# The conditioning table of the first stage in parts of 512 columns, four tiles at a time

## The reference

```python
cond = jax.nn.silu(c)                        # c: (1, 1024)
for l in range(DEPTH):
    mod = cond @ w_ada[l] + b_ada[l]         # w_ada[l]: (1024, 9 * 1024)
    sh1, sc1, g1, sh2, sc2, g2, sh3, sc3, g3 = jnp.split(mod, N_MOD, axis=-1)
    h = modulate(rms_norm(x), sh1, sc1)
    x = x + 0.5 * g1[:, None, :] * swiglu(h, w_ff1_in[l], w_ff1_out[l])
    ...
```

## Time and profile before

| | |
|---|---|
| median of 3 runs | 3588.3 us (3585.97 to 3589.84) |
| span of the profiled execution | 3586.1 us |
| PE busy | 3451.8 us (96%) |
| DVE, ACT, POOL busy | 1818.5, 1210.8, 643.6 us |
| moved by DMA | 357.82 MB, 100 GB/s in the mean |
| the table's 16 parts | 512 KB each, 8.7 us from issue to landing (median) |

### The profile page before, as it was taken

The page is one execution under the profiler, slowest core; times in us unless marked ns, Lnnn a source line. Parts: engine busy times, 40 slices in busy tenths (PEclk is TensorE's granted clock), DMA queues, the critical chain, the costliest instruction groups (busy, mean ns, idle before and its releaser), DMA issues. The chain is left out here.

```text
span 3586.1 us, 49320 instructions
## 1 busy us (share of the span) xinstructions
PE 3451.8 (96%) x20618; PEld 2725.1 (76%) x20618; DVE 1818.5 (51%) x2601; ACT 1210.8 (34%) x1729; POOL 643.6 (18%) x438
## 2 busy tenths in 40 slices
PE   7999999989999999999998899999899999989999
PEld 5888774577888788877558688878678887778887
DVE  6777536745454566663574533336643335363332
ACT  4222334544222322233364422232542223253223
POOL 4202111131202120211013120220021210001112
PEclk9999999999999999999999999999999999999999
DMA  7565321003443346542000223222132223123321
GB/s 232 162 208 170 124 72 36 7 27 105 128 154 116 120 155 198 157 137 84 32 10 27 83 88 107 87 87 83 36 106 94 95 94 97 48 71 96 104 94 59
DMA packets 445201, 357.82 MB, mean 100 GB/s; under 512 B 15990, under 2 KB 441012, under 8 KB 444980
## 3 DMA queue, kind: packets, MB, share of 16 engines
q1 hardware_dynamic: 444980, 354.67, 31.5%
HBM read 350.43 MB, written 2.10 MB: 98 GB/s over the span
## 5 line engine op out<-in xcount | busy, mean ns | idle before, releaser
L600 DVE TENSOR_TENSOR ring_wlo<-ring_raw,ring_whi 128x2048 fp32r<-128x2048 f32 (+3 forms) x268 | 570.8, 2130 | 377.2 <-ACT ring_whi L581 346.5
L581 ACT ACTIVATE ring_whi<-ring_raw 128x2048 fp32r<-128x2048 f32 (+3 forms) x278 | 490.4, 1765 | 649.3 <-PE f_ps L1099 242.9
L1097 PE MATMUL f_ps<-act_hi,ring_whi 128*128 128x512 f32 x1280 | 502.0, 392 | 2.5 <-DVEq L1251 2.5
L1099 PE MATMUL f_ps<-act_hi,ring_wlo 128*128 128x512 f32 x1280 | 498.7, 390 | 0.0
L1098 PE MATMUL f_ps<-act_lo,ring_whi 128*128 128x512 f32 x1280 | 498.0, 389 | 0.0
L1207 POOL TENSOR_TENSOR f_glo<-f_v,f_ghi 128x512 fp32r<-128x512 f32 x88 | 237.7, 2701 | 1035.2 <-ACT f_ghi L1199 1035.2
L1189 ACT ACTIVATE f_t<-f_ps 128x512 f32<-128x512 f32 x88 | 52.6, 598 | 692.8 <-PE f_ps L1099 648.4
L1097 PEld LDWEIGHTS f_ps<-act_hi,ring_whi 128*128 128x128 f32 x1280 | 240.3, 188 | 52.3 <-DVEq L1251 3.8
L1099 PEld LDWEIGHTS f_ps<-act_hi,ring_wlo 128*128 128x128 f32 x1280 | 240.2, 188 | 50.7
L1098 PEld LDWEIGHTS f_ps<-act_lo,ring_whi 128*128 128x128 f32 x1280 | 240.5, 188 | 49.0
L1097 PE MATMUL f_ps<-f_ghi,ring_whi 128*128 128x512 f32 x704 | 277.0, 393 | 0.0
(11 more groups left out here) (596 smaller groups left out, 5908.9 us busy)
## 6 DMA issues: line engine op xcount, KB each, us to landing
ring_raw<-in_w_ff_in SPq DMA_DIRECT2D x176, 512.0 KB, 4.8
f_ada_raw<-in_w_ada SPq DMA_DIRECT2D x128, 512.0 KB, 5.5
ring_raw<-in_w_mlp SPq DMA_DIRECT2D x64, 1024.0 KB, 5.1
ring_raw<-in_w_in SPq DMA_DIRECT2D x42, 1024.0 KB, 5.2
ring_raw<-in_w_ff_out SPq DMA_DIRECT2D x32, 768.0 KB, 4.7
ring_raw<-in_w_ff_out SPq DMA_DIRECT2D x32, 640.0 KB, 4.4
ring_raw<-in_w_out SPq DMA_DIRECT2D x16, 1024.0 KB, 5.3
ada_raw<-in_w_ada SPq DMA_DIRECT2D x16, 512.0 KB, 8.7
```

Source lines behind the costliest of these rows:

```text
L581: eng.activation(self.w_hi[:, i % self.SPLIT, 0:s.nk, 0:w], self.raw[:, i % self.RAW, 0:s.nk, 0:w], ACT.Copy)\
L600: eng.tensor_tensor(self.w_lo[:, i % self.SPLIT, 0:s.nk, 0:w], self.raw[:, i % self.RAW, 0:s.nk, 0:w], self.w_hi[:, i % self.SPLIT, 0:s.nk ...
L1097: eng.matmul(out, wh, o_hi[:, a, :], start=(s.first and q == 0), stop=False)
L1099: return eng.matmul(out, wl, o_hi[:, a, :], start=False, stop=(s.last and q == s.nk - 1))
```

## The change

A subclass `Quads` takes the place of `Side` in the first stage. A quad is four tiles (512 columns); there are 4. A part is 2 k-tiles by 512 columns, again 512 KB, in rows of 2 KB, and a quad has 4 parts. The ring stays at 10 buffers. Row sum, keep, turn and take each handle a quad, and `first_sums` adds four columns.

The order changes too. On PE row sum 0 stands behind all transposes, and both halves of the squares follow before anything else of the table; then come turn 0, row sum 1, the vectors, turn 1, row sum 2, turn 2, row sum 3 and turn 3. On DVE keeps 0 and 1 stand before the vectors, takes 0 and 1 behind them, then keep 2, the chunk masks, `take_lo` of slot 0, take 2, keep 3 and take 3. On SP the sequence is as before; part 10 and later ones wait for the k-tiles of the new, smaller parts.

```diff
--- before.py
+++ after.py
@@ -110,7 +110,7 @@
         sq = sb("sq", [P, DT, S])
         ps = [ctx.enter_context(nc.psum_tensor(f"ps_const{i}", [P, 512], F32)) for i in (0, 1, 2, 3)]
         small, sums = ps[3][:, 0:24], ps[1:3]
-        side = Side(nc, k, ctx, "ada0", rest[:Side.SEMS + ring], *first, ring)
+        side = Quads(nc, k, ctx, "ada0", rest[:Side.SEMS + ring], *first, ring)
         rest = rest[Side.SEMS + ring:]
         vecs = [Vectors(nc, k, ctx, f"vec0{i}", rest[Vectors.SEMS * i:Vectors.SEMS * (i + 1)], *v)
                 for i, v in enumerate(vectors)]
@@ -122,16 +122,14 @@
             eng.dma_start(pos_i[:, :], bcast_rows(k.inp["positions"], P)).then_inc(pload, 16)
             eng.dma_start(inv[:, :], inv_freq).then_inc(pload, 16)
             eng.dma_start(xin[:, :, :], k.inp["x"].rearrange("b (t p) d -> p (b t) d", p=P)).then_inc(xload, 16)
-            for s in range(5):
-                side.load(eng, s)
+            side.load_parts(eng, range(10))
             for v in vecs:
                 v.load(eng)
             eng.dma_start(rows[0:8, :], k.inp["final_norm_g"].rearrange("(r p) -> r p", p=P)).then_inc(load, 16)
             eng.dma_start(rows[8:16, :], k.inp["final_norm_g_2"].rearrange("(r p) -> r p", p=P)).then_inc(load, 16)
-            side.load(eng, 5)
+            side.load_parts(eng, range(10, 12))
             k.ring.load(eng, 0)
-            for s in range(6, side.pairs):
-                side.load(eng, s)
+            side.load_parts(eng, range(12, 16))
             for i in range(1, 1 + Ring.RAW):
                 k.ring.load(eng, i)
 
@@ -245,13 +243,11 @@
                 if t >= 3:
                     eng.wait_ge(xdone, t - 2)
                     eng.wait_ge(squared, t - 2)
-                if t == 5:
-                    eng.wait_ge(cdone, 2)
-                    side.row_sum(eng, 0, wide)
                 for j in range(4):
                     mm = eng.transpose(ps[t % 3][:, j * P:(j + 1) * P], xin[:, j, t * P:(t + 1) * P], k.ident)
                 mm.then_inc(xt, 1)
-            side.row_sum(eng, 1, wide)
+            eng.wait_ge(cdone, 2)
+            side.row_sum(eng, 0, wide)
             eng.wait_ge(squared, DT)
 
             def squares(first):
@@ -260,21 +256,18 @@
                 if first:
                     mm.then_inc(summed, 1)
 
+            squares(0)
+            squares(DT // 2)
             side.row_turn(eng, 0, sums, pick)
-            side.row_sum(eng, 2, wide)
-            side.row_turn(eng, 1, sums, pick)
-            squares(0)
-            side.row_sum(eng, 3, wide)
-            squares(DT // 2)
+            side.row_sum(eng, 1, wide)
             for v in vecs:
                 v.turn(eng)
             eng.wait_ge(load, 32)
             eng.transpose(small[:, 0:16], rows[:, :], k.ident[0:16, 0:16]).then_inc(turned, 1)
-            side.row_turn(eng, 2, sums, pick)
-            for s in range(4, side.pairs):
+            side.row_turn(eng, 1, sums, pick)
+            for s in (2, 3):
                 side.row_sum(eng, s, wide)
-                side.row_turn(eng, s - 1, sums, pick)
-            side.row_turn(eng, side.pairs - 1, sums, pick)
+                side.row_turn(eng, s, sums, pick)
 
         @block.scalar
         def _(eng):
@@ -348,7 +341,7 @@
             then(eng.tensor_tensor(turns[:, :, :], turns[:, :, :], over[:, :, :], ALU.add))
             eng.tensor_scalar(turns[:, :, :], turns[:, :, :], lim, -lim, ALU.min, ALU.max).then_inc(folded, 1)
 
-            for t in range(4):
+            for t in range(2):
                 side.row_keep(eng, t)
             for v in vecs:
                 v.copy(eng)
@@ -356,15 +349,14 @@
                 v.end(eng)
             eng.wait_ge(turned, 2)
             eng.tensor_copy(k.finals, small[:, 0:16]).then_inc(cdone, 1)
-            for t in range(3):
+            for t in range(2):
                 side.row_take(eng, t, sums)
-            for t in range(4, side.pairs):
-                side.row_keep(eng, t)
-                side.row_take(eng, t - 1, sums)
-                if t == 5:
-                    chunk_masks()
-                    k.ring.take_lo(eng, 0)
-            side.row_take(eng, side.pairs - 1, sums)
+            side.row_keep(eng, 2)
+            chunk_masks()
+            k.ring.take_lo(eng, 0)
+            side.row_take(eng, 2, sums)
+            side.row_keep(eng, 3)
+            side.row_take(eng, 3, sums)
 
 
 def np_pi():
@@ -509,6 +501,54 @@
         eng.tensor_reduce(part, ps, AX, ALU.add).then_inc(self.reduced, 1)
         eng.wait_ge(self.reduced, b + 1)
         self.finish(eng, 4 * b, part).then_inc(self.taken, 1)
+
+
+class Quads(Side):
+
+
+    TWO, PART = 4 * P, KC // 4
+
+    def __init__(self, nc, k, ctx, name, sems, l, tiles, finish, ring):
+        super().__init__(nc, k, ctx, name, sems, l, tiles, finish, ring)
+        self.quads = len(tiles) // 4
+
+    def load_parts(self, eng, parts):
+
+        for j in parts:
+            if j >= self.ring:
+                eng.wait_ge(self.step, self.PART * (j - self.ring + 1))
+            col, row = self.tiles[j // 4 * 4] * P, j % 4 * self.PART * P
+            w = self.k.inp["w_ada"][bass.ds(self.l, 1), row:row + self.PART * P, col:col + self.TWO]
+            eng.dma_start(self.raw[:, j % self.ring, :, :], w.rearrange("a (q p) n -> p (a q) n", p=P))\
+               .then_inc(self.landed[j % self.ring], 16)
+
+    def row_sum(self, eng, s, wide):
+
+        if s >= 2:
+            eng.wait_ge(self.reduced, s - 1)
+        for q in range(KC):
+            j = 4 * s + q // self.PART
+            if q % self.PART == 0:
+                eng.wait_ge(self.landed[j % self.ring], 16 * (j // self.ring + 1))
+            at = q % 4 * 32
+            mm = eng.matmul(self.ps[s % 2][at:at + 32, 0:self.TWO], wide[:, q, :],
+                            self.raw[:, j % self.ring, q % self.PART, :], start=(q < 4), stop=(q >= KC - 4))
+            mm.then_inc(self.step, 1)
+
+    def row_turn(self, eng, s, out, pick):
+
+        eng.wait_ge(self.reduced, s + 1)
+        if s >= 2:
+            eng.wait_ge(self.taken, s - 1)
+        for c in range(4):
+            mm = eng.matmul(out[s % 2][:, c:c + 1], self.acc[:, s % self.accs, c * P:(c + 1) * P], pick[:, :],
+                            start=True, stop=True)
+        mm.then_inc(self.turned, 1)
+
+    def row_take(self, eng, s, out):
+
+        eng.wait_ge(self.turned, s + 1)
+        self.finish(eng, 4 * s, out[s % 2][:, 0:4]).then_inc(self.taken, 1)
 
 
 class Slot:
@@ -3626,7 +3666,7 @@
             return lambda eng, at, ps: finished(eng, slice(first + at, first + at + 4), ps)
 
         def first_sums(eng, at, ps):
-            return finished(eng, slice(at, at + 2), ps)
+            return finished(eng, slice(at, at + 4), ps)
 
         def start_layer(eng, halved, groups=3):
```

## The result

The changed kernel takes 3591.5 us (median of 20 runs) against 3587.0 for the kernel before beside it (20 runs): the ratio is 1.0015, with a 95% interval of 1.0009 to 1.0021. The forecast of 3586.6 was a gain of 1.7 us; what came is a loss of 4.5 us between the two medians, and of 0.15% (some 5.4 us) by the ratio: within the 0.2% forecast with 0.95, and half a microsecond above the range. The profiled execution of after has a span of 3590.6 us against 3586.1. Each kernel left one profiled execution, and every time inside a kernel is read from that one.

What follows compares the result with a forecast made beforehand. Bound by matmuls on PE, except in a first stage of some 46 us. That stage ending at 44.35 instead of 46.04 takes 1.7 us off the median 3588.3, giving 3586.6; range 3583.5 to 3591, eight in ten.

Steps and rivals of the forecast that it cites:

- The stage: First stage: squares at full clock, masks 2.15 us earlier, stage end at 44.35 against 46.04, 1.7 us won.
- the prediction's upper bound: First stage: at most 2.6 us won, with parts landed early and the last turn at full clock; 3585.7 us.
- Why the clock held: Squares on PE: full clock assumed, as idle time ahead shrinks to about 0.4 us; otherwise a half-rate stretch costs 1.76 us.
- The transfers and the tail: First stage's loads and end: landing taken as unchanged, keep 3 at about 41.5, stage end at 44.35.
- Row length doesn't show in the rate: First-stage loads: 349 GB/s with 1 KB rows, 356 with many of 512 B, so the landing stays as it is.
- the 358 that the prediction set against a faster table: First-stage loads: memory-side limit of about 358 GB/s for a core; the landing would come only 0.1 us earlier.
- the two k-tiles of the last part: Row sum 3 on PE: work left after the last landing, some 0.5 us, so keep 3 can start at about 41.5.
- The late landing: Rival, first-stage tail: last parts land after 42.6 and delay keep 3; 3589.5 us, chance 0.12.
- Nothing later runs by absolute time, and so a microsecond won or lost at 46.04 should reach the end as a microsecond: Everything behind the first stage: its whole gain of 1.7 us comes off the span, 3586.1 to 3584.4.
- It does nothing for the end: Rival, feed-forward start: it could wait for something unmoved, its second weight slot; 3588.3 us, chance 0.24 shared with another rival.

Runs made afterwards that it cites:

- the kernel with the late load: Changed kernel, 2 MB of weights loaded in mid chunk stage now issued only when PE has finished that stage: 3588.9 us against 3588.2, ratio 1.0000.
- four other kernels: Kernel before with 119 empty PE instructions (3591.7 us); changed kernel with 256 empties (3598.4), rows of 1 KB (3593.0), or row sum 1 before the squares (3591.5).
- the 137 split empties: Changed kernel plus empty PE instructions, 100 before the wait for x and 37 after row sum 3, restoring old block edges: 3587.6 us against 3588.2, ratio 1.0000.
- The version with both: Changed kernel with 137 empty PE instructions (100 and 37) and the mid-chunk weight loads held back until PE finishes that stage: 3585.9 us against 3587.2, ratio 0.9997.

## Why the prediction was wrong, point by point

*The stage: right.* Squares unbroken at clock 1.00 for 7.13 us from 20.21 (forecast 7.08 from 19.97). A row sum 1.92 (2.0), a copy 0.69 (0.69), a turn of four 0.95 to 1.05 (1.1), the last turn 1.87 at half clock, as forecast. Masks at 34.87, the floor that POOL's row had set at 34.87; DVE free at 41.30 (41.35). First scaling 44.44 (44.7), first weight product 47.00 (46.9). Gain 1.95 (1.7). How much it is hangs on the clock of the last turn: in the kernel with the late load, whose first stage is the same, it took 1.08 us at full clock, and the gain was 2.62, the prediction's upper bound.

*Why the clock held: the reason isn't shown.* The forecast put the full clock down to the missing idle time ahead of the squares. With row sum 1 first there were 0.98 us of idle time and the clock held too; but that is less than the 1.26 us of before, so the idle time is not excluded. Which difference to the kernel before kept the clock up is open.

*The transfers and the tail: two terms mis-sized, in opposite directions.* "Row length doesn't show in the rate" rested on one pair of stretches, with a mix of rows in the second. Rows of 2 KB moved at 388 GB/s against 349: the last part was used at 37.91, not about 40.9. 388 GB/s is also above the 358 that the prediction set against a faster table, so that limit did not hold here. The other way, the two k-tiles of the last part took 1.05 us and not 0.5. In after neither shows, as DVE was busy until 41.30. With rows of 1 KB, where the table came as late as the sum had it, the last copy started at 42.48 and not at 41.5: that this part of the sum came out in after is luck. The late landing, the rival on the slower side, was off in the same direction.

*"Nothing later runs by absolute time, and so a microsecond won or lost at 46.04 should reach the end as a microsecond": the step that failed.* The first half is not contradicted: 1.90 of the 1.95 us were still there at 1825, though with −1.27 and −2.30 on the way. But the step left out that the change shortens PE's instruction stream. The loss is +7.4 us in the second layer: 2.8 of it are longer stops at the edges (5.31 − 2.56), and the greater part of the rest is the half clock behind them (the 4.0 us in the output piece). With the load moved, after kept the full clock there and lost 3.0. That the stops let the clock fall is inferred from this order of events, which four other kernels repeat in the chunks; no kernel stopped PE alone, and with the 137 split empties the clock fell once in the output piece (0.74 from 1985 to 1990 us) without a long stop at an edge.

*The rivals.* "It does nothing for the end" is nearest to the outcome, but it named a wait of the feed-forward that does not move; the loss lay 1900 us behind, in no wait that the trace of before names with a releaser. No rival took in the stream's length, though the page of before has the queue and the earlier trace rows the count of matmuls.

*The size.* With the old edges, after is at 1.0000 (0.9991 to 1.0009), and with the late load too at 0.9997 (0.9988 to 1.0006). The forecast ratio, 1 − 1.7 / 3588.3 = 0.9995, lies in both intervals, and so does 1. The version with both is faster than after, as the intervals of the two don't meet, and not measurably faster than before. The 2 us of the stage are in the traces; that they reach the end was not shown, as the differences move by up to another 2.4 us behind 2003. What sizes the stops at an edge, between 0.2 and 2.4 us, is open as well: in the chunks 256 instructions last about 4 us and the blocks mostly come 3.4 to 4.4 us apart, so there is hardly any lead, but why the new edges are worse by themselves wasn't settled.

## What to carry to other kernels

An edit that adds or takes away instructions moves every block edge behind it, so where a stage of many short matmuls follows, look for waits with no releaser and follow the difference between the traces through the whole kernel before the edit is blamed. Empty instructions in an idle gap can put the edges back, and are the control that tells the edit from its shift. A stage on which only a few microseconds hang can be forecast to a few tenths from rows, and still say little of the end.

## What the runs showed of the hardware

PE's instructions come in blocks of 16.4 KB, 256 instructions, through a DMA queue, and in a stage of some 60 instructions in a microsecond PE stops at their edges: 2.56 us in 100 in the kernel before, up to 6.66 in others. It went on 2.2 to 2.9 us after the start of the block's transfer. The Trainium skill, "Runtime: NRT & Kernel Launch", Instruction fetch mechanics, gives the same blocks and calls the cost of crossing an edge mostly hidden; the trace agrees for the block, and for this stage it doesn't for the cost.

A load of 2 MB in flight held one such block up: 6.6 us from the block before it instead of about 4 (7.5 in the kernel before), and the stop of 1.84 us behind it vanished when the load was moved.

Loads from memory went in at 388 GB/s with rows of 2 KB and at 349 with rows of 1 KB, in the same ten microseconds of the same stage.

An empty instruction on PE took 0.074 us: with 256 of them the transposes began at 21.41, with 137 at 12.56, so (21.41 − 12.56) / 119.
